# RWKV-7 and gated DeltaNet recurrences: two products with equal weights become one of 128 columns, and RWKV's loop over chunks is written out

## What is computed

```
lmat = where(i > s, (beta*k) @ k.T * decay, 0)
tmat = triangular_solve(lmat + eye, eye)        # inverse of a unit lower triangle
u = tmat @ (v * beta);  w = tmat @ (beta*k * exp(gc))
# over the chunks, with state s:
v_new = u - w @ s
o = q_in @ s + qk @ v_new
s = s * exp(g_last) + k_out.T @ v_new
```

```
sa = S a_t;   S = S diag(w_t) + sa b_t^T + v_t k_t^T;   o_t = S r_t
```

## Time and profile before

| | |
|---|---|
| median of 3 runs | 3762.94 us (3762.4 to 3763.13) |
| the profiled execution | 3761.25 us, its span 3759.3 us |
| TensorE (PE) busy | 3450.2 us, 92% of the span |
| weight loads (PEld) busy | 3290.5 us |
| DVE, ACT, POOL busy | 1804.4, 1101.0 and 1114.9 us |
| DeltaNet's recurrence | from about 384 to 596 us of the span |
| RWKV's recurrence | from about 2318 to 2645 us |

### The profile page before, as it was taken

How to read it: one execution, slowest core, us unless ns; L and a number is a source line. 1 busy time by engine, 2 the same in 40 slices (tenths; PEclk the granted TensorE clock), 3 DMA queues, 4 the chain that set the end, 5 groups by cost and what they waited for, 6 DMA issues and landing times.

```text
span 3759.3 us, 76537 instructions
## 1 busy us (share of the span) xinstructions
PE 3450.2 (92%) x32526; PEld 3290.5 (88%) x32526; DVE 1804.4 (48%) x2237; ACT 1101.0 (29%) x1660; POOL 1114.9 (30%) x506
## 2 busy tenths in 40 slices
PE   8999797999999999899988877888799999999989
PEld 7988686999999999899987445877789999999989
DVE  1562553665444444754411226333367444544474
ACT  2365453331111112321022335333242112111141
POOL 2332312543333333333322000000244333333323
PEclk9999898999999999999998998999999999999999
DMA  3111002211111111122211013001211111111111
GB/s 132 49 60 53 8 0 101 62 48 42 45 45 39 45 45 39 52 73 80 91 60 49 1 51 99 18 18 59 86 57 49 42 45 45 39 45 45 39 46 74
DMA packets 69648, 194.75 MB, mean 52 GB/s; under 512 B 23328, under 2 KB 24608, under 8 KB 68832
## 3 DMA queue, kind: packets, MB, share of 16 engines
q1 hardware_dynamic: 57536, 150.76, 12.8%
q10 hardware_dynamic: 11936, 41.34, 2.9%
HBM read 163.82 MB, written 28.25 MB: 51 GB/s over the span
## 4 chain that ended last, share of the span: by engine, by line
PE 82%; DVE 8%; ACT 5%; issue 4%; ACTq 0%; DMA 0%; POOL 0%; DVEq 0%; SPq 0%; POOLq 0%; PEldq 0%
PE PS L747 54%; PE PS L764 11%; PE PS L1002 7%; PE PS L779 2%; PE PS L1396 1%; PE PS L1012 1%; DVE XL L2370 1%; PE PS L1374 1%; PE PS L1442 1%; PE PS L1371 1%; PE PS L1485 1%; ACT XH L1750 1%; DVE Y L2364 1%; PE PS L1356 0%; ACT Y L1752 0%
## 5 line engine op out<-in xcount | busy, mean ns | idle before, releaser
L859 POOL TENSOR_TENSOR WHI<-RAW,EPS 128x1024 fp32r<-128x1024 f32 x234 | 452.7, 1935 | 2440.0 <-PE PS L747 1349.0
L747 PE MATMUL PS<-XH,WHI 128*128 128x274 f32 x3936 | 1142.2, 290 | 11.5 <-ACT RN L1622 6.3
L747 PE MATMUL PS<-XL,WHI 128*128 128x274 f32 x3936 | 1141.6, 290 | 0.0
L747 PE MATMUL PS<-XH,WLO 128*128 128x274 f32 x3936 | 1139.8, 290 | 0.0
L747 PEld LDWEIGHTS PS<-XH,WHI 128*128 128x128 f32 x3936 | 743.9, 189 | 14.4 <-issue 9.0
L747 PEld LDWEIGHTS PS<-XL,WHI 128*128 128x128 f32 x3936 | 745.3, 189 | 0.0
L747 PEld LDWEIGHTS PS<-XH,WLO 128*128 128x128 f32 x3936 | 744.9, 189 | 0.0
L862 POOL TENSOR_TENSOR WLO<-RAW,WHI 128x1024 fp32r<-128x1024 f32 x234 | 606.0, 2590 | 18.3
L747 PE MATMUL PS<-HH,WHI 128*128 128x274 f32 x1280 | 372.0, 291 | 0.4 <-DVE Y L2456 0.3
L747 PE MATMUL PS<-HH,WLO 128*128 128x274 f32 x1280 | 370.4, 289 | 0.0
L747 PE MATMUL PS<-HL,WHI 128*128 128x274 f32 x1280 | 369.4, 289 | 0.0
(11 more groups left out here) (476 smaller groups left out, 5487.2 us busy)
## 6 DMA issues: line engine op xcount, KB each, us to landing
RAW<-in_units SPq DMA_DIRECT2D x234, 512.0 KB, 3.5
c_rows<-DX ACTq DMA_DIRECT2D x14, 548.0 KB, 2.7
RKV<-c_rows SPq DMA_DIRECT2D x4, 1644.0 KB, 9.7
X<-in_x SPq DMA_DIRECT2D x8, 548.0 KB, 9.0
XR<-in_x ACTq DMA_DIRECT2D x8, 548.0 KB, 12.6
bonus_gate_rows<-BG SPq DMA_DIRECT2D x4, 1096.0 KB, 5.0
XR<-x_rows ACTq DMA_DIRECT2D x8, 548.0 KB, 7.0
CIN<-c_rows SPq DMA_DIRECT2D x34, 128.0 KB, 3.0
```

The lines of the kernel that those rows point to most:

```text
L747: last = nc.tensor.matmul(PS[:, 4 * slot + b, 0:width], wt[:, ring, w], r[:, k, b * width:(b + 1) * width], start=n == 0, stop=n == 3 * nk ...
L859: nc.gpsimd.tensor_tensor(WHI[:, s, :], RAW[:, s, :], ZERO.to_broadcast([128, 1024]), ALU.add)\
```

## The change

Levels 1 to 3 of both inverses issue `g` and `tt` as one product: weights N, moving G and TT side by side in one tile (GT_B, GT_S), 128 columns per head, into one whole PSUM bank; ACT copies the bank out with one ACTIVATE of 512 columns. A level that follows such a product waits for that one copy before its first product; before, its first product waited only for the copy of G and its third for that of TT. Level 4 drops its second wait. In DeltaNet level 1 waits for TT's first copy (tt1) ahead of its first product.

RWKV's loop is written out in Python on every engine, on SP too; DeltaNet's loop stays a hardware loop.

```
-            with eng.Fori(1, count) as i:
-                if loop_start:
+            if loop_start:
+                with eng.Fori(1, count) as i:
                     loop_start(i)
-                together((i, 0), 0, (i, -1), 1)
-                together((i, 0), 1, (i, 0), 0)
-            if loop_end:
+                    together((i, 0), 0, (i, -1), 1)
+                    together((i, 0), 1, (i, 0), 0)
                 loop_end()
+            else:
+                for i in range(1, count):
+                    together((0, i), 0, (0, i - 1), 1)
+                    together((0, i), 1, (0, i), 0)
...
-            with sp.Fori(0, 7) as i:
+            for i in range(7):
...
-        LEVEL = [("a", "g", "tt")] * 4 + [("a", "tt"), ("tt",)]
+        LEVEL = [("a", "g", "tt")] + [("a", "gt")] * 3 + [("a", "tt"), ("tt",)]
...
+        NGT = both("NGT", 4, 192)
+        G_S = [NGT[p][:, :, 64:128] for p in range(2)]
+        TT_S = [NGT[p][:, :, 128:192] for p in range(2)]
+        GT_S = [NGT[p][:, :, 64:192] for p in range(2)]
+        N_S = [[NGT[p][:, :, 0:64], N_ODD[p]] for p in range(2)]
...
                     if level < 5:
-                        pe.wait_ge(c_act[p], C_ACT.at(j, "g%d" % level if level else "bt"))
+                        pe.wait_ge(c_act[p], C_ACT.at(j, ("bt", "g1", "gt2", "gt3", "gt4")[level]))
                         tiled()
                         c_heads(stacked(b), G_S[p], n).then_inc(s, 1)
-                    if level < 4:
+                    if level == 0:
                         c_heads(stacked(b + 3), n, G_S[p]).then_inc(s, 1)
-                    if level == 1:
-                        pe.wait_ge(c_act[p], C_ACT.at(j, "kt"))
-                    elif level:
-                        pe.wait_ge(c_act[p], C_ACT.at(j, "tt%d" % level))
-                    if level:
+                    elif level < 4:
+                        c_heads(per_head(b + 3), n, GT_S[p]).then_inc(s, 1)
+                    elif level == 4:
+                        c_heads(stacked(b + 2), n, TT_S[p]).then_inc(s, 1)
+                    else:
+                        pe.wait_ge(c_act[p], C_ACT.at(j, "tt5"))
                         tiled()
                         c_heads(stacked(b + 2), n, TT_S[p]).then_inc(s, 1)
...
-                        out, bank = (G_S, 4 * p + 3) if x == "g" else (TT_S, 4 * p + 2)
-                        nc.scalar.activation(out[p][:, :, :], stacked(bank), ACT.Copy).then_inc(s, 1)
+                        out, product = {"g": (G_S, stacked(4 * p + 3)), "gt": (GT_S, per_head(4 * p + 3)),
+                                        "tt": (TT_S, stacked(4 * p + 2))}[x]
+                        nc.scalar.activation(out[p][:, :, :], product, ACT.Copy).then_inc(s, 1)
```

More of the change, by code:

```diff
@@ L317, in build @@
         BLOCK_LEVEL = at("BLOCK_LEVEL", [128, 6, 64], spare)
-        TT_B = [at("TT_B%d" % p, [128, 4, 64], spare + 1536 + 1024 * p) for p in range(2)]
+        A_B = [at("A_B%d" % p, [128, 4, 64], spare + 1536 + 1024 * p) for p in range(2)]
         ABOVE = at("ABOVE", [128, 128], spare + 1536 + 2048)
-        G_B = [at("G_B%d" % p, [128, 4, 64], SETS[p][7]) for p in range(2)]
-        A_B = [at("A_B%d" % p, [128, 4, 64], SETS[p][7] + 1024) for p in range(2)]
+        GT_B = [at("GT_B%d" % p, [128, 4, 128], SETS[p][7]) for p in range(2)]
+        G_B = [GT_B[p][:, :, 0:64] for p in range(2)]
+        TT_B = [GT_B[p][:, :, 64:128] for p in range(2)]
         WW_B = [at("WW_B%d" % p, [128, 4, 64], SETS[p][9]) for p in range(2)]
@@ L403, in build @@
         ARI = both("ARI", 4, 192)
[L404 to L408, removed]
+        B_S, K_S, N_ODD, AK_S, BT_S, KT_S, VT_S, PI_S, RB_S, RK_S, X_S, U_S = [both(x, 4, 64) for x in (
+            "B_S", "K_S", "N_ODD", "AK_S", "BT_S", "KT_S", "VT_S", "PI_S", "RB_S", "RK_S", "X_S", "U_S")]
+        NGT = both("NGT", 4, 192)
[3 more added lines that the diff above has]
+        N_S = [[NGT[p][:, :, 0:64], N_ODD[p]] for p in range(2)]
         PX = both("PX", 4, 65)
@@ L620, in build @@
         C_LEVEL = [("a", "g")] + LEVEL[1:]
-        C_KEPT = [("g",)] + KEPT_OF[1:]
+        C_KEPT = [[x for x in parts if x != "a"] for parts in C_LEVEL]
         C_PE = ChunkStages("vt", "l", "lt", "kg", "bg", *[x + str(l + 1) for l in range(6) for x in C_LEVEL[l]], "x", "u", "o", "m")
@@ L672, in tile_place, with in_loop, in_line @@
             return ds(8 * j[0] + (8 * j[1] + 4 * p), 4)
+        def in_loop(i):
+            pass
+        def in_line():
+            pass
         def run_chunks(eng, do, first_half=FIRST, second_half=SECOND, sample=C_SAMPLE, loop_start=None, loop_end=None):
@@ L828, in _ @@
             sp.dma_start(MB[1][:, :, :], io["s_c"]).then_inc(c_state_in, 16)
-            with sp.Fori(0, 7) as i:
+            for i in range(7):
                 for p in range(2):
-                    sp.wait_ge(c_pe[p], C_PE.at((i, 0), "vt"))
-                    sp.wait_ge(c_dve[p], C_DVE.at((i, 0), "rs"))
-                    load_tokens(p, chunk_columns((i, 1), p))
+                    sp.wait_ge(c_pe[p], C_PE.at((0, i), "vt"))
+                    sp.wait_ge(c_dve[p], C_DVE.at((0, i), "rs"))
+                    load_tokens(p, chunk_columns((0, i + 1), p))
             sp.wait_ge(c_pe[0], C_PE.at((0, 7), "vt"))
@@ L1047, in g_step @@
                     if l < 5:
-                        pe.wait_ge(gdn_act[p], G_ACT.at(j, "g%d" % l))
+                        pe.wait_ge(gdn_act[p], G_ACT.at(j, ("g0", "tt1", "gt2", "gt3", "gt4")[l]))
                         tiled()
                         c_heads(stacked(b + 3), G_B[p], n).then_inc(s, 1)
-                    if l < 4:
+                    if l == 0:
                         c_heads(stacked(b + 1), n, G_B[p]).then_inc(s, 1)
-                    if l == 0:
                         pe.wait_ge(gdn_dve[p], G_DVE.at(j, "qk"))
-                    else:
-                        pe.wait_ge(gdn_act[p], G_ACT.at(j, "tt%d" % l))
-                    tiled()
-                    c_heads(stacked(b + 2), n, TT_B[p] if l else PAIR_ID).then_inc(s, 1)
+                        tiled()
+                        c_heads(stacked(b + 2), n, PAIR_ID).then_inc(s, 1)
+                    elif l < 4:
+                        c_heads(per_head(b + 1), n, GT_B[p]).then_inc(s, 1)
+                    elif l == 4:
+                        c_heads(stacked(b + 2), n, TT_B[p]).then_inc(s, 1)
+                    else:
+                        pe.wait_ge(gdn_act[p], G_ACT.at(j, "tt5"))
+                        tiled()
+                        c_heads(stacked(b + 2), n, TT_B[p]).then_inc(s, 1)
                 elif name == "w6":
@@ L1667, in g_step @@
                         act.wait_ge(gdn_pe[p], G_PE.at(j, stage))
-                        out, bank = (G_B, b + 1) if x == "g" else (TT_B, b + 2)
-                        nc.scalar.activation(out[p][:, :, :], stacked(bank), ACT.Copy).then_inc(s, 1)
+                        out, product = {"g": (G_B, stacked(b + 1)), "gt": (GT_B, per_head(b + 1)), "tt": (TT_B, stacked(b + 2))}[x]
+                        nc.scalar.activation(out[p][:, :, :], product, ACT.Copy).then_inc(s, 1)
                 elif name == "w6":
@@ L2707, in c_step @@
                     dve.wait_ge(s, C_DVE.at(j, "masked"))
-                    nc.vector.tensor_tensor(NG[p][:, :, :], NG[p][:, :, :], PAIR_ID.unsqueeze(1).to_broadcast([128, 8, 64]), ALU.add)\
+                    ng = NGT[p][:, :, 0:128].rearrange("p m (g n) -> p g m n", g=2)
+                    nc.vector.tensor_tensor(ng, ng, PAIR_ID.unsqueeze(1).unsqueeze(1).to_broadcast([128, 2, 4, 64]), ALU.add)\
                         .then_inc(s, 1)
```

8 lines of the change are left out of this document (4 added, 4 removed).

## The result

The changed kernel takes 3727.56 us (median of 4 runs, 3726.32 to 3735.8) against 3762.67 us for the kernel before beside it (4 runs, 3760.87 to 3763.13): a ratio of 0.9912, 95% interval 0.9895 to 0.9929, or 35.1 us less. I had forecast 3743 and a range down to 3732. The sign was right and the size was not. The profiled execution took 3726.32, its span 3724.5.

What follows compares the result with a forecast made beforehand. PE, busy 92% of the span, was taken to bound the kernel, so only time between its products counts. The terms -38.5 + 19.1 - 0.4 = -19.8 us from 3762.9 gave 3743 us, range 3732 to 3757.

Steps and rivals of the forecast that it cites:

- Term 1: RWKV's loop written out removes the fetch wait behind the back edge in six long passes: 38.5 us gain.
- Term 2: Merged product on PE, levels 1 to 3 of both recurrences: each merge saves 0.06 us of PE.
- Term 3: RWKV's merged copy on ACT ends later: +0.64 us at l2 to l3, +0.49 at l3 to l4; sum +19.1.
- DeltaNet's term: DeltaNet's merges: later copy stays hidden, 1.6 us gained on PE less about 1.2 in the first chunk: -0.4 us.
- The clock did not fall in RWKV's new gaps: Rival: the clock falls once in each RWKV pass's new gaps, +18 us, 3761, no change; chance 0.09.
- The branch isn't the cause: Rival: writing out RWKV's loop gains nothing, 3782; chance 0.03.
- The merge is hidden after all: Rival: RWKV passes have unseen slack, so only the written-out loop counts, 3721; chance 0.06.
- The fetch comes late without a branch too: Rival: 14 written-out RWKV passes lose 3.4 us each to late instruction fetches, 48 us, 3791; chance 0.08.
- Theory (C): Rival set after the result: the written-out loop and the merge aren't independent; no size or chance given.

Runs made afterwards that it cites:

- e1_out: Kernel before with RWKV's loop written out and no product merged anywhere: 3717.53 us against 3767.01, ratio 0.9867.
- e6_one_out: Kernel before with RWKV's loop written out and only RWKV's level 1 merged, DeltaNet as before: 3712.02 us against 3764.00, ratio 0.9859.
- e2: Changed kernel with RWKV's hardware loop put back, merges of both recurrences kept: 3731.91 us against 3767.01 for the kernel before, ratio 0.9913.
- e8: Changed kernel with RWKV's loop kept and its merged products issued as two of 64 columns, one wait and copy: 3780.88 us, ratio 1.0044 to before.
- e10: Kernel before with RWKV's loop written out and RWKV's levels 1 and 2 merged, DeltaNet as before: 3727.93 us against 3763.49, ratio 0.9905.
- e9: Kernel before with RWKV's loop written out and RWKV's levels 1 and 3 merged, DeltaNet as before: 3727.70 us against 3763.49, ratio 0.9898.
- e7: Changed kernel with RWKV's hardware loop put back and DeltaNet's levels unmerged as before: 3729.43 us against 3764.00 for the kernel before, ratio 0.9902.
- e4: Changed kernel with RWKV's merged product copied out in two pieces, G first, next level waiting for G alone: 3729.47 us, ratio 0.9900 to before.
- e3: Changed kernel, loop written out, RWKV's merged products issued as two of 64 columns, one wait and copy kept: 3735.25 us, ratio 0.9916 to before.
- e11: Kernel before with RWKV's levels 1 and 3 merged, its loop kept, DeltaNet as before: 3746.64 us against 3763.49, ratio 0.9958.
- e5: Kernel before with only RWKV's level 1 merged, its loop kept, DeltaNet as before: 3759.62 us against 3764.00, ratio 0.9990.

## Why the forecast was off

**Term 1 was mis-sized, and it is the step that failed.** I wrote that the same position in the order, "run straight through (the loop's first pass), takes 16.42", and took that as the pass without a fetch. It had no gap of 3 us, but a late block of 0.48, and PE busy for 15.24 us where e1_out's clean pass shows 14.70 with about as many instructions; I passed over both. The clean pass is 15.49 (e1_out). With it the fifteen passes of before sum to 298.66 - 14.59 = 284.07, and 15 x 15.49 = 232.4: 51.7 us to be had, of which the six long passes hold 137.03 - 6 x 15.49 = 44.1 and the nine short ones 7.6. Straight code can have nearly all of it: the fifteen passes of e6_one_out sum to 232.57. The changed kernel lost only 1.6 us to late blocks, so it had 50.1 of the 51.7 where term 1 had 38.5. These 11.6 us are most of the 16.9 by which RWKV beat its forecast (36.3 against 38.5 - 19.1 = 19.4). My upper end of 40.5 came from the shortest pass shown, 16.1, which was no clean pass either, and it left the nine short passes out.

The number 38.5 was not far off for the loop alone in one execution: e1_out's profiled one has a mean pass of 16.44, since it kept 14.2 us of late blocks. What was wrong is to take these blocks for the pass's own work, to add the merge's price on top of them, and so to carry them into a kernel that has hardly any.

**That the fetch at the back edge is the cause was right.** e1 takes the branch away and the gaps go; e2 keeps the branch, makes the body fit, and the gaps go; e8 keeps the branch and the waits of e2, makes the body long, and the gaps are back. These runs carry the point better than my reading of the earlier trace rows did: of its two gaps only the second, 1.96, stands inside a group; the first, 3.33, stands ahead of it, where a wait would stand too. The Trainium skill ("Runtime: NRT & Kernel Launch", Instruction fetch mechanics) has a taken branch wait for a fetch when its target is outside the current window of two pages. The trace agrees that a target which isn't held costs a fetch, but not on the window: by that section two pages are 512 instructions, and e2's body of 1552 matmuls and loads was held.

**Term 2 was right:** 0.06 us for a merge on PE (15.49 to 15.43; 16.65 to 16.48 with three).

**Term 3 was right in its mechanism and nearly in its size.** Forecast +0.64 and +0.49 a pass, measured +0.62 (e10) and +0.47 (e9). Level to level is 2.29, not 2.35. In all, the changed kernel has 16.9 us less gain than e6_one_out (52.0 - 35.1). The terms forecast 19.1 + 1.0 - 0.4 = 19.7 between these two, since e6 keeps the merge of l1 and has none in DeltaNet.

**DeltaNet's term had the wrong sign.** The forecast was -0.4; the recurrence is 1.9 us longer in the profile. I left out the sample's chain at its end (1.2 us) and one fall of the clock more (1 us). The same two falls stand in e2's profile, and the one of before in those of e1, e6 and e7.

**The sum again,** in RWKV's fifteen passes of the profiled execution: 51.7 of room, less 15 x (16.48 - 15.49) = 14.9 for the merge, less 1.6 for the three late blocks, is 35.2; the passes went from 284.07 to 248.77, by 35.3. The last stretch of RWKV gives 1.0 more (14.59 to 13.56) and DeltaNet takes 1.9, which makes 34.4 of the span's 34.8.

**The rivals.** The clock did not fall in RWKV's new gaps of 0.94 and 0.38: it is 1.00 in every pass. "The branch isn't the cause" is refuted. "The merge is hidden after all" gave the number nearest to the result, 3721, and is wrong all the same: the clean pass is 0.99 us longer with the merges, and e1 and e6, without the merges of l2 and l3, are 14 and 17 us better by the medians (4 and 16 in RWKV's part of the profiles). "The fetch comes late without a branch too" is true, and my reason against it was a misreading: I wrote that the loop's first two passes show no late block, and they show three. Its price was 0.2 to 1.6 us for a block beside the loads of tokens, where I had set 3.4, and 2.6 to 4.1 beside the loads of 2.2 MB (e1, e9, e10). Part of it had been in the kernel before as well. Theory (C) is right in two ways: both parts cure the same wait, and the late blocks, 14.2 us in e1_out's profile, are 1.6 in the changed kernel's.

**What the change amounts to.** Each of its parts does away with the back edge's wait, one by taking the branch out and one by shrinking the body, so the second adds nothing: 35.1 with both, 35.1 with the merges alone (e2), 49.5 with the loop alone. (In the profiles RWKV's recurrence takes 262.33, 263.91 and 258.18 us.) The better version is e6_one_out, written out and merged only at l1, where other work covers the copy: 3712.02, a ratio of 0.9859 (0.9843 to 0.9875).

**Left open.** That the short gaps are late fetches like the long ones rests on their place inside a group and on e2, where they end once the body is held. Why late blocks fall into some variants' passes more than others' was not settled. Over their fifteen passes they cost 14.2 us in e1, 10.2 in e9, 9.0 in e10, 3.0 in e4, 2.8 in e3, 1.6 in the changed kernel and 1.1 in e6, in one profiled execution each. The number of instructions doesn't order them: e1 and e3 have 873 and 876 a pass, e6 has 844. Where a block border lies in the order and what is on the queues then are the candidates, and no run moved the one without the other. The exact size that is held lies between 1552 and 1688 matmuls and loads, with the waits and branches that have no rows on top. Why e11 waits at every second back edge and not at each was not tried either. The spread of single runs (3726.32 to 3735.8 for the changed kernel, 3741.75 to 3753.32 for e11) is large beside the differences among e2, e3, e4 and the changed kernel, which I therefore don't rank.

## What to carry to other kernels

Before pricing the removal of a stall, look for the same stall in a small form in the passes that you take as clean; a short pass is not yet a free one, and PE's busy time and the gaps inside groups tell them apart. Count a hot loop's instructions per engine: a few per cent can decide whether each iteration is fetched anew, and then either a smaller body or straight code cures it, but not twice. Merge products with equal weights where other work stands before their readers; side by side with the next level, the wait for the longer copy costs eight to ten times what the merge saves (0.47 and 0.62 against 0.06).

## What the runs showed of the hardware

- One loop on PE, four sizes, and three behaviours: held (1552), fetched again at every second back edge (1624), at every one (1688 and more). A miss costs a gap of 3.1 to 4.8 us, in most cases a second one of 0.3 to 2.8, and a clock of 0.73 to 0.92 in that pass: from 21.69 - 15.99 = 5.7 us (e11) over 22.09 - 15.57 = 6.5 to 25.43 - 15.57 = 9.9 (e5). Before, it was 44.1 / 6 = 7.4.
- Straight code of 64 by 64 fp32 products, some 55 matmuls and loads per us (844 in 15.43), outran its fetch by 0.2 to 1.6 us at a block now and then, with 0.10 of the DMA share in use, and by 2.6 to 4.1 us once in each of e1, e9 and e10 beside 221 to 242 GB/s of other loads. In e6_one_out the pass beside 232 GB/s was clean at 15.43: the traffic alone does not decide.
- A loop that is held is not quite free: e2_merge's pass takes 16.61, the same pass written out 16.48.
